# The front of a two-block transformer kernel: w_ada by column quarters and w_in by row quarters, in turns

## What is computed

```
mod = jax.nn.silu(c) @ w_ada + b_ada                      # w_ada: 2048 x 12288
shift1, scale1, gate1, shift2, scale2, gate2 = jnp.split(mod, N_MOD, axis=-1)
h = modulate(rms_norm(x, norm1_w), shift1, scale1)        # h*(1+scale)+shift
p = h @ w_in                                              # w_in: 2048 x 4112
u_f = p[..., :o1]; q_in, k_in, v_in = ...; o_gate = sigmoid(...); gates = p[..., o5:] + b_gates
y_f = fourier_mix(u_f)
y_m = mlstm_bidirectional(q_in, k_in, v_in, gates, mlstm_norm_w) * o_gate
x = x + gate1 * (concatenate([y_f, y_m]) @ w_out)
h2 = modulate(rms_norm(x, norm2_w), shift2, scale2)       # then a feed-forward with gate2
```

## Time and profile before

| | us |
|---|---|
| median of 3 runs | 3562.35 (3561.05 to 3566.18) |
| the profiled execution, its own time | 3561.49 |
| its span in the profile | 3559.6 |
| TensorE busy | 3403.8 (96%) |
| VectorE busy | 2017.6 (57%) |
| ScalarE busy | 1528.3 (43%) |
| chain that ended last: TensorE | 79% of the span |
| chain that ended last: loads of w_ada into the stage | 3% |

### The profile page before, as it was taken

How to read it: one execution, slowest core, us unless ns; L and a number is a source line. 1 busy time by engine, 2 the same in 40 slices (tenths; PEclk the granted TensorE clock), 3 DMA queues, 4 the chain that set the end, 5 groups by cost and what they waited for, 6 DMA issues and landing times.

```text
span 3559.6 us, 45278 instructions
## 1 busy us (share of the span) xinstructions
PE 3403.8 (96%) x18458; PEld 2863.0 (80%) x18458; DVE 2017.6 (57%) x2010; ACT 1528.3 (43%) x1554; POOL 346.1 (10%) x411
## 2 busy tenths in 40 slices
PE   5899889999999999999999899999999999999998
PEld 1786678888888888888888799898888788888886
...
GB/s 398 296 340 311 219 172 224 223 223 226 189 187 192 189 196 177 207 199 197 193 189 189 166 150 157 168 174 249 86 96 191 175 189 189 189 190 190 190 190 139
DMA packets 543073, 713.09 MB, mean 200 GB/s; under 512 B 13127, under 2 KB 382079, under 8 KB 535360
## 3 DMA queue, kind: packets, MB, share of 16 engines
...
## 4 chain that ended last, share of the span: by engine, by line
PE 79%; DVE 9%; ACT 4%; DMA 4%; issue 3%; POOL 1%; ACTq 0%; SPq 0%; DVEq 0%; POOLq 0%
PE ps L2585 9%; PE ps L2587 9%; PE ps L2586 9%; PE ps L2443 9%; PE ps L2444 8%; PE ps L2447 8%; PE ps L2375 7%; PE ps L2376 3%; DVE w_lo L1372 3%; ACT w_hi L812 3%; DMA stage<-in_w_ada 3%; PE ps L2394 2%; PE ps L2396 2%; PE ps L2395 2%; PE ps L2407 1%
## 5 line engine op out<-in xcount | busy, mean ns | idle before, releaser
L1372 DVE TENSOR_TENSOR w_lo<-stage,w_hi 128x2048 fp32r<-128x2048 f32 x528 | 1221.4, 2313 | 1176.0 <-ACT w_hi L812 1175.2
L812 ACT ACTIVATE w_hi<-stage 128x2048 fp32r<-128x2048 f32 x528 | 1010.7, 1914 | 1567.3 <-PE ps L2587 575.9
L2585 PE MATMUL ps<-w_hi,xt 128*128 128x512 f32 x1408 | 552.3, 392 | 3.4 <-DVE xt L1423 1.8
L2586 PE MATMUL ps<-w_lo,xt 128*128 128x512 f32 x1408 | 549.6, 390 | 0.0
L2587 PE MATMUL ps<-w_hi,xt 128*128 128x512 f32 x1408 | 549.6, 390 | 0.0
L2375 PE MATMUL ps<-xt,w_hi 128*128 128x512 f32 x1320 | 472.3, 400 | 6.2 <-DVE w_lo L1372 6.2
L2443 PE MATMUL ps<-w_hi,hid_hi 128*128 128x512 f32 x1152 | 449.6, 390 | 5.9 <-DVE w_lo L1372 5.9
L2444 PE MATMUL ps<-w_lo,hid_hi 128*128 128x512 f32 x1152 | 448.3, 389 | 0.0
L2376 PE MATMUL ps<-xt,w_lo 128*128 128x256 f32 x1320 | 371.3, 281 | 0.0
L2394 PE MATMUL ps<-xt,w_hi 128*128 128x256 f32 x1184 | 342.9, 290 | 18.6 <-DVE w_lo L1372 16.0
L2447 PE MATMUL ps<-w_hi,hid_lo 128*128 128x512 f32 x1152 | 354.6, 389 | 0.0
...
## 6 DMA issues: line engine op xcount, KB each, us to landing
stage<-in_w_in SPq DMA_DIRECT2D x92, 1024.0 KB, 5.7
stage<-in_w_up SPq DMA_DIRECT2D x88, 1024.0 KB, 5.7
stage<-in_ffn_w_gate SPq DMA_DIRECT2D x88, 1024.0 KB, 5.1
stage<-in_ffn_w_up SPq DMA_DIRECT2D x88, 1024.0 KB, 5.1
stage<-in_ffn_w_down SPq DMA_DIRECT2D x88, 1024.0 KB, 5.4
stage<-in_w_ada SPq DMA_DIRECT2D x48, 1024.0 KB, 8.7
stage<-in_w_down SPq DMA_DIRECT2D x44, 1024.0 KB, 5.5
...
```

Of the source, the lines that this page charges most:

```text
L812: act.activation(w_hi[:, u % 2 * UNIT:(u % 2 + 1) * UNIT], slot(u % SLOTS), ACT.Copy).then_inc(hi_made, 1)
L1372: dve.tensor_tensor(w_lo[:, part], slot(u % SLOTS), w_hi[:, part].bitcast(F32), ALU.subtract).then_inc(split_made, 1)
L2585: pe.matmul(dst, chunk(xt_hi, k, m), wh, start=k == 0, stop=False)
L2586: pe.matmul(dst, chunk(xt_hi, k, m), wl, start=False, stop=False)
```

## The change

- The first 64 units of the stream come in a new order. shift1 and scale1 are made in four quarters of 512 output columns: eight units of w_ada each (512 rows x 512 columns, four for shift1 and four for scale1). Quarter q gives the modulation of input columns 512q to 512q+511, which is all that rows 512q to 512q+511 of w_in need. w_in comes in 32 units of 512 rows x 512 columns, eight for each quarter of rows.
- The order is: 8 units of w_ada; three times 16 units in which the 8 w_in units of quarter q (`IN_PLACE`) and the 8 w_ada units of quarter q+1 (`ADA_PLACE`) take turns; then the last 8 w_in units with nothing between.
- The product of a unit covers a quarter of K only, so each unit's result (two banks) is taken out of PSUM: ACT copies those of quarter 0 (`first_part`), DVE adds those of quarters 1 to 3 into SBUF (`add_part`), 48 additions of 128x512.
- shift2 moves from the late pieces to the stream: 32 units of w_ada for shift2 and scale2 (`ada2`), all of them between the Fourier part's groups and the heads, where 16 stood. The next load of this kind waits until TensorE has used the unit four before it.
- Late pieces: only the 32 of gate1 are left, in a ring of two buffers. DVE takes 8 of them beside the last w_in quarter, 8 in the Fourier part, 4 in the heads, and 12 in `out1` (two after unit 1, two before unit 4, two after each of units 4 and 5, four after unit 6). gate1 is folded and turned around unit 7 of `out1`, TensorE waits for it before unit 8, and the gated add goes from unit 9 to unit 13.
- The sigmoid of the output gate is one ScalarE instruction of 128x2048 behind the Fourier part, as the projection now ends in SBUF.

Core of the diff (the definitions `way`, the copies of gate rows and the waits that are only renumbered are left out):

```diff
+IN_PLACE = (0, 2, 4, 6, 9, 12, 14, 15)
+ADA_PLACE = (1, 3, 5, 7, 8, 10, 11, 13)
...
-    late_ring = [sb("late0", HALF, at=FN + 8192), sb("late1", HALF, at=OV + 41024),
-                 sb("late2", HALF, at=RB + 4096), sb("late3", HALF, at=FN + 4096)]
+    late_ring = [sb(f"late{k}", HALF, at=XN + 8192 + 4096 * k) for k in range(2)]
...
# SP
+        def fetch(at, src, whole, count, used):
+            if freed[at % SLOTS]:
+                sp.wait_ge(*freed[at % SLOTS])
+            dst = slot(at % SLOTS)
+            sp.dma_start(dst if whole else dst.rearrange("p (k n) -> p k n", k=4), src).then_inc(landed[at % SLOTS], 16)
+            freed[at % SLOTS] = (used, count)
+        def fetch_ada(a):
+            q, i = divmod(a, 8)
+            col = i // 4 * D + q * 512
+            fetch(ada_place(a), ada_parts[i % 4][:, :, col:col + 512], False, a + 1, S["ada_used"])
+        def fetch_in(n):
+            q, i = divmod(n, 8)
+            fetch(in_place(n), in_parts[q][:, :, i * 512:(i + 1) * 512], False, n + 1, split_made)
...
# POOL
+        pool.wait_ge(S["norm_turned"], 8)
+        for n in range(2, 32):
+            pool.wait_ge(S["late_acc"], n - 1)
+            late_piece(n)
+        pool.wait_ge(S["mod_made"], 7)
+        pool.dma_start(gates_dram[0].rearrange("(k p) -> p k", p=P), mod[:, 32:48]).then_inc(S["to_dram"], 16)
...
# DVE
+        def add_part(n):
+            dve.wait_ge(split_used, n + 3)
+            dve.wait_ge(S["tile_copied"], max(8, n - 7))
+            for h in range(2):
+                last = dve.tensor_tensor(part_of(n, h), part_of(n, h), part_bank(n, h), ALU.add)
+            last.then_inc(S["tile_copied"], 1)
...
+        for n in range(32):
+            q, i = divmod(n, 8)
+            if n >= 10:
+                add_part(n - 2)
+            if i == 0:
+                quarter_scale(q)
+            split_in(n)
+            if i == 0:
+                quarter_lo(q)
+            if q == 3:
+                late(i, 1)
...
             rest(duo(xt_lo, g), turned_duo(g), duo(xt_hi, g), S["mix_lo"])
+            late(8 + 2 * g, 2)
+            if g == 1:
+                dve.wait_ge(S["ec_made"], 1)
+                dve.tensor_copy(ecols[:, :], bank(3, 0, 32)).then_inc(S["ec_copied"], 1)
+                copy_sum(7, 0, ADA + KC)
+        take_sum(3, bank(3, 64, 16), 5)
...
+        late(22, 2)
         for u in range(4, 16):
             split("out1", 16, 0, u)
-            if u == 9:
+            if u < 6:
+                late(16 + 2 * u, 2)
+            elif u == 6:
+                late(28, 4)
+            elif u == 8:
+                copy_sum(7, 0, ADA + 2 * KC + 1)
+            elif u == 9:
+                take_sum(2, bank(7, 0, 16), 7)
+            if u == 13:
...
# TensorE
+        for q in range(3):
+            for step in range(16):
+                if step in IN_PLACE:
+                    i = IN_PLACE.index(step)
+                    in_unit(8 * q + i)
+                    if i == 2:
+                        norm(0, range(2 * q + 2, 2 * q + 4))
+                    elif i == 6:
+                        turn_quarter(q + 1)
+                else:
+                    ada(8 * (q + 1) + ADA_PLACE.index(step))
+        for i in range(8):
+            in_unit(24 + i)
...
+            for v in ((0, 1, 2, 3, 4), (5, 6, 7, 8), (9, 10, 11, 12), (13, 14, 15, 16))[g]:
+                ada2(v)
+            if g == 3:
+                turn_sum(3, 64, 0, 5)
...
-                scale_units(10 + 2 * h, 2)
+                for v in ((17, 18, 19, 20, 21, 22, 23), (24, 25, 26, 27), (28, 29, 30, 31))[h]:
+                    ada2(v)
...
-        rows_half("out1", 8, 0, 0, at_out1, units=range(2, 8), ready=S["mix_lo"])
+        rows_half("out1", 8, 0, 0, at_out1, units=range(2, 7), ready=S["mix_lo"])
+        pe.wait_ge(S["late_acc"], 32)
+        fold_rows(7, late_acc[0][:, :])
+        rows_half("out1", 8, 0, 0, at_out1, units=range(7, 8), ready=S["mix_lo"])
+        turn_sum(7, 0, 0, 7)
+        pe.wait_ge(S["mod_made"], 7)
         rows_half("out1", 8, 1, 8, at_out1 + 8, quarters=True)
```

More of the change, by code:

```diff
@@ L70, in stream_plan @@
 def stream_plan():
-    order = [("in_tiles", 16, 16), ("in_rows", 16, 16), ("ada2", KC, 0), ("out1", 16, 16)]
+    order = [("in", 32, 32), ("ada2", 2 * KC, 0), ("out1", 16, 16)]
     def ffn(n):
@@ new lines, in quarter_hi @@
+        def quarter_hi(q):
+            act.wait_ge(S["mod_made"], q + 1)
+            for g in (2 * q, 2 * q + 1):
+                act.wait_ge(S["norm_turned"], g + 1)
+                if g >= 2:
+                    act.wait_ge(S["norm_done"], g - 1)
+                c = 2 * g + 1
+                link.then(act.activation(turn[:, g % 2 * 512 + T:(g % 2 + 1) * 512], bank(5, g % 2 * T, T),
+                                         ACT.Identity, scale=scale_cols[:, c:c + 1], bias=mod[:, c:c + 1]))
+                act.wait_ge(S["norm_scaled"], g + 1)
+                act.activation(duo(xt_hi, g), turned_duo(g), ACT.Copy).then_inc(S["norm_hi"], 1)
@@ L1798, in _ @@
-        dve.wait_ge(S["ec_made"], 1)
-        dve.tensor_copy(ecols[:, :], bank(2, 0, 32)).then_inc(S["ec_copied"], 1)
-        copy_sum(3, 0, ADA + 2)
+        for n in (30, 31):
+            add_part(n)
+        dve.wait_ge(S["f_act"], 2)
+        link.then(dve.scalar_tensor_tensor(out=two(lfrow[:, :]), in0=fgates, scalar=0.0,
+                                           in1=two(crow[:, :]), op0=ALU.min, op1=ALU.subtract))
+        for d in range(2):
+            last = dve.tensor_tensor_scan(way(rows1, 2 + d, d), ones1[:, :], way(lfrow, d, d), 0.0,
+                                          ALU.mult, ALU.add)
@@ L1801, in _ @@
+        link.then(last)
+        link.then(dve.tensor_tensor(two(rows1[:, 0:512]), igates, two(rows1[:, 512:1024]), ALU.subtract))
+        for d in range(2):
+            last = dve.tensor_tensor_scan(way(rows1, 4 + d, d), ones1[:, :], way(rows1, d, d), NEG,
+                                          ALU.mult, ALU.max)
+        link.then(last)
+        dve.tensor_tensor(rows1[:, 512:1024], rows1[:, 512:1024], rows1[:, 1024:1536],
+                          ALU.add).then_inc(S["f_dve"], 1)
         for g in range(4):
@@ L2670, in _, with turn_quarter, ada @@
-        ada(0, 12)
+        def turn_quarter(q):
+            pe.wait_ge(S["mod_summed"], q + 1)
+            for b in range(2):
+                for t in range(4):
+                    last = pe.matmul(bank(6 + b, t, 1), mod_row[b][:, t * P:(t + 1) * P], four_rows[:, :],
+                                     start=True, stop=True)
+            last.then_inc(S["mod_turned"], 1)
+        def ada(a):
+            q, i = divmod(a, 8)
+            at = ada_place(a)
+            pe.wait_ge(landed[at % SLOTS], 16 * (at // SLOTS + 1))
+            if i == 0:
+                pe.wait_ge(*((S["mod_made"], q) if q else (S["csilu_made"], 1)))
+            for kk in range(4):
+                k = 4 * (i % 4) + kk
+                last = pe.matmul(ps[32 * kk:32 * kk + 32, (6 + i // 4) * 512:(7 + i // 4) * 512],
+                                 csilu[:, k:k + 1].to_broadcast([P, 32]), slot(at % SLOTS)[:, kk * 512:(kk + 1) * 512],
+                                 start=i % 4 == 0, stop=i % 4 == 3)
+            last.then_inc(S["ada_used"], 1)
```

417 lines of the change are left out of this document (204 added, 213 removed).

## The result

| | before | after |
|---|---|---|
| median of 4 runs each (us) | 3562.96 | 3610.14 |
| lowest to highest | 3561.05 to 3566.18 | 3606.69 to 3614.81 |
| profiled execution, its own time | 3561.49 | 3612.05 |

The ratio is 1.0132 with a 95% interval of 1.0115 to 1.015: slower by 47 us, where the forecast was slower by 20 and its range ended at 3596. The sign was right and the size was not.

The account below looks back on a forecast made before the run. The prediction took the first 108.5 us as bound by loading w_ada, then TensorE as the bound to 387 us. Terms -41.1, +46.4 and +14.6 gave +19.9: a median of 3582 us, range 3570 to 3596.

Parts of the forecast that it names:

- A: Start of the kernel to the first matmul with w_in: forecast to fall from 108.5 to 43.7 us.
- B: Projection, first to last matmul: length from 209.0 to 232.7 us, its end earlier by 41.1 us.
- the bound of -31: Projection's end at its slow bound: each slot wait half as long again, plus a pause at each change of quarter.
- I put 3 us once for the low clock: Projection: one allowance of 3 us for TensorE's low clock at the start.
- rival 3: TensorE's pauses of 2 us and more bring back half clock: +20 us, 3602 us in all; chance 0.2.
- where a w_in unit follows a w_ada unit in its slot: Projection: the slot is free only after TensorE's use, then 9.8 us to refill; waits of 4.3 us a quarter.
- C: Last projection matmul to out1: from 69.6 to 116 us, +46.4, with 32 w_ada units standing there.
- The upper bound, +50: Last projection matmul to out1, with scores twice at the slower pitch seen after a pause: +50 us.
- D: out1: +14.6 us, from late pieces around units 4 to 7, the fold and unit 8's wait for mod.
- The bound for this, +19: out1, if the clock is low for some us after each of the two 4.5 us pauses: +19 us.
- Rival 1: Faster: quicker landings in the quarters, and DVE's wait ends before the load queue runs dry; 3553 us, chance 0.17.
- Nothing: The single sigmoid, the additions, the larger program and the loads' 2 KB rows were forecast to cost nothing.

Follow-up runs that it names:

- e12: e9 with the load of the first w_in unit of each group, except the first group, moved ahead of its two w_ada units; 3589.0 us.
- e4: Changed kernel with other places in a quarter, so only one w_in unit soon follows a w_ada unit in its slot; 3612.3 us.
- e9: Changed kernel with the order in a quarter set to two w_ada units, two w_in units, four times; 3599.3 us.
- e5: Changed kernel with four of head 0's w_ada units taken straight behind the Fourier part, ahead of TensorE's wait for mod; 3597.1 us.
- e3: Changed kernel with four buffers in place of two for the late pieces of out1 (pieces 20 to 31); 3603.2 us.
- e6: Changed kernel with eight of the 32 shift2 and scale2 units taken in turns with the last eight w_in units; 3602.0 us.
- e11: e10 with e12's load order, no late pieces beside a quarter's first and last w_in units, last two scale2 units beside the last head's product; 3538.7 us.
- e10: Changed kernel with e1, e5, e6 and e9's order joined, late pieces beside all w_in units, gate1 folded in the Fourier part; 3571.4 us.
- e1: Changed kernel with VectorE's copy of shift2's sum moved from behind the second Fourier group's work to behind the third's; 3608.6 us.

## Why the prediction was right and wrong

**A, the start: right, with some luck.** 44.7 for 43.7. The last w_ada unit ended at 36.7 where 34.3 was taken, and from there it was 8.0 us where 9.4 was; the two errors nearly cancel.

**B: the mechanism right, the size short by 10.2.** The slot waits were 13.2 us for 12.9, though not by places: 2.1 on average at step 9 for 2.0, none at step 12 for 1.5, and 2.4 at step 14 for 0.8. The end of B moved by -29.9, just beyond the bound of -31. Two things were missed. First, the term "I put 3 us once for the low clock": half-clock stretches, 1.5 to 1.7 us each, came not once but five times, at the start and behind four of the six waits (78.07, 96.47, 152.89, 214.77), 8.2 us in sum. Quarters with a clock of 0.92 and 0.97 stand above. Rows at both levels lay in the earlier trace rows; I used them for rival 3 and left them out of the sum. Second, the pitch of a unit: 5.85 to 5.95 where 5.76 was taken, 5.57 to 5.67 where 5.44, a w_ada unit 0.99 where 0.93: about 1.6 a quarter, as each change between the kinds of unit cost 0.1 to 0.2 (in pairs, as in e12, two w_ada units took 1.85). And the step "where a w_in unit follows a w_ada unit in its slot" was only half of the reason for the waits: e4 and e9 show that they stay in part without it, and e12 that the other half is the order of SP's loads.

**C: the places right, short by 13.6.** Counted from the end of the projection, the copy of shift2's sum came at 48.8 (49.3 forecast), `mod` at 63.8 (61.3), the first unit of the heads at 72.0 (67.3), the landing that ended the dry queue at 80.8 (72.7), the last unit's use at 111.8 (100.7), and 17.8 more to out1 (15.1). From the copy to `mod` it was 15.0 where 12.0 was taken, as VectorE waited 4.2 for a late piece to land. The step "scores 2.2, exponents 1.7, scores 2.2" was late by 2.2: behind 9.9 us of waiting the four rows ran at half clock and took 8.0 in all. The landing was late by 3.4: the slot came free after a unit at half clock (1.9, left out of the forecast) and the load took 6.8, not 5.3. The chain of landings from there was late by 3.0, of which 1.0 is the last unit at half clock. The product of head 2 with `v_one` took 4.87 where 2.87 stood, that of head 3 took 5.33 where 4.55 stood. So about half of the 13.6 is work at half clock and the other half landings. The upper bound, +50, was too low by 10, as it varied one of these alone. That held slots, and not only VectorE's wait, make the dry queue is shown by e5; how much of C the half clock costs is read from the rows and was not tested.

**D: short by 4.7.** Forecast 14.6, measured 19.3. The waits were as named (unit 4 late by 1.25 for 1.4, the fold 4.87 for 4.6, unit 8 3.68 for 4.5). From unit 4 to unit 8 it was 37.7 us where 21.7 stood before, so 16.0 for 13.2, and behind unit 8 another 2.1: the 2.8 and the 2.1 beyond the forecast go with matmuls at half clock, 0.91 in the mean of out1 where 0.98 stood. The bound for this, +19, was the value.

**Behind out1**, 1.5 us that no term had: the transposes of the second normalisation at half clock. No run ties them to the waits of out1: the stretch is 18.2 us long in e3 and e6, which have such waits, and 19.7 to 19.9 in the others, e11 among them.

**The rivals.** Rival 3 gave 3602 by "TensorE's pauses of 2 us and more bring the half clock back" and had the nearest number (the forecast's last line has it "beyond 3603", which its own 3602 is not; both lie above the range). It had priced twelve waits at 1.7, or 20; where TensorE bounds, the half clock took 5.2 beyond the 3 in B, up to 4.7 in D and 1.5 behind it, or 11. Its place was right in part, its size was not, and C's 13.6, half of it landings, brought the rest. My argument against it, "in the tile phase all later pauses passed at 1.00", rested on one stage of a kernel with one long pause in it, and four of six pauses here went the other way; in e10 none of six did, so neither the argument nor the rival's rule holds for every such pause. The Trainium skill (TensorE: Matmul & The Clock Gate, "HAM oscillation"), which advises for thin matmuls to do all of K before waiting for loads, spoke for it. On that rule the trace agrees in that waits matter, with 0.92 and 0.97 in the quarters that have them and 0.99 in e12, which has K cut in the same way and no waits; the 1.00 of e10, which has waits, does not fit it. Rival 1, faster, is not this kernel. e11 comes near to what it described, with 2.7 us of waits in B, but it gets there by moving units and pieces too, and its queue does run dry.

**Nothing: held, with its condition.** The sigmoid cost nothing under the wait for `mod`, and its end 1.8 us when e1 took the wait away. The additions cost nothing: in e12 TensorE was busy for 219.06 of 219.10 us with them beside it.

The failing step is one kind of step in every stage but A: each wait was costed at its own length, and the work and the loads behind it at the pitch of an undisturbed stretch. In the forecast's terms, the low clock was put at 3 us once, where it took 8.2 in B, some 7 in C, up to 4.7 in D and 1.5 behind it; the landings in C took some 6.5 more than 5.3 and 2.46 a load gave; and the pitches of B were short by 4.8. That the half clock comes with waits in this kernel is read from its rows; why it comes behind some and not behind others stays open.
